# Moving the next layer's sixteen first modulation columns from the second-table stage to between the output projection panels

## The reference, cut to what matters

```python
c_act = jax.nn.silu(c)
for l in range(DEPTH):                       # DEPTH = 2
    mod = c_act @ w_mod[l] + b_mod[l]        # w_mod[l]: 1024 x 6144
    sh1, sc1, g1, sh2, sc2, g2 = jnp.split(mod, 6, axis=-1)
    h = _modulate(_rmsnorm(x), sh1, sc1)
    z = h @ w_in[l]
    ...                                      # gating, latent attention, pooling: ya, yb, yc
    merged = (gates[:, :, 0] * (ya @ w_a[l]) + gates[:, :, 1] * (yb @ w_b[l])
              + gates[:, :, 2] * (yc @ w_c[l]))
    x = x + g1[:, None, :] * (merged @ w_o[l])
    h2 = _modulate(_rmsnorm(x), sh2, sc2)
    x = x + g2[:, None, :] * _peer(h2, w_pq[l], sub_keys[l], u_tab[l], v_tab[l])
return _rmsnorm(x, final_norm)
```

## Time and profile before

| | |
|---|---|
| time, median of 3 runs | 3391.51 us (3388.35 to 3396.68) |
| the profiled execution | 3398.23 us, of which span 3396.4 us |
| PE busy | 3335.4 us, 98% of the span |
| DVE busy | 2685.5 us, 79% |
| ACT busy | 1400.9 us, 41% |
| POOL busy | 1451.2 us, 43% |
| granted clock of PE, mean | 0.987 of 2.4 GHz |
| HBM, mean over the span | 267 GB/s |

### The profile page before, as it was taken

How to read it: one execution, slowest core, us unless ns; L and a number is a source line. 1 busy time by engine, 2 the same in 40 slices (tenths; PEclk the granted TensorE clock), 3 DMA queues, 4 the chain that set the end, 5 groups by cost and what they waited for, 6 DMA issues and landing times.

```text
span 3396.4 us, 51667 instructions
## 1 busy us (share of the span) xinstructions
PE 3335.4 (98%) x16944; PEld 2905.3 (86%) x16944; DVE 2685.5 (79%) x4905; ACT 1400.9 (41%) x2298; POOL 1451.2 (43%) x1291
## 2 busy tenths in 40 slices
PE   7999999999999999999999999999999999999999
PEld 5777789999999988888877767999999998888887
DVE  6455668999888689999854556799998877899996
ACT  3334343434477433333343342443435773333333
POOL 1011106766662345566301101086767524456661
PEclk9999999999999999999999999999999999999999
DMA  6475437767799999999734744477768999999994
GB/s 228 134 253 187 150 121 221 213 206 230 228 309 327 349 393 378 399 404 402 304 129 148 241 158 154 144 221 215 214 205 260 337 320 379 361 405 399 405 400 184
DMA packets 306395, 909.86 MB, mean 268 GB/s; under 512 B 69076, under 2 KB 101892, under 8 KB 305316
## 3 DMA queue, kind: packets, MB, share of 16 engines
q0 software_dynamic: 163792, 473.58, 40.6%
q1 hardware_dynamic: 105552, 383.83, 31.8%
q10 hardware_dynamic: 36868, 50.35, 4.1%
HBM read 792.14 MB, written 115.47 MB: 267 GB/s over the span
## 4 chain that ended last, share of the span: by engine, by line
PE 91%; DVE 4%; DMA 2%; issue 1%; POOL 1%; ACT 1%; ACTq 0%; SPq 0%; DVEq 0%; POOLq 0%
PE ps L462 15%; PE ps L464 15%; PE ps L463 15%; PE ps L1076 11%; PE ps L1074 10%; PE ps L1075 10%; PE ps L1054 3%; PE ps L877 2%; PE ps L974 1%; PE ps L975 1%; PE ps L976 1%; PE ps L933 1%; PE ps L506 1%; PE ps L1014 1%; DVE urow L1693 1%
## 5 line engine op out<-in xcount | busy, mean ns | idle before, releaser
L462 PE MATMUL ps<-mov,whl 128*128 128x384 f32 (+1 forms) x2816 | 1007.7, 358 | 1.2 <-DVE whl L449 1.2
L464 PE MATMUL ps<-mov,whl 128*128 128x384 f32 (+1 forms) x2816 | 987.6, 351 | 0.0
L463 PE MATMUL ps<-mov,whl 128*128 128x384 f32 (+1 forms) x2816 | 987.0, 350 | 0.0
L449 DVE TENSOR_TENSOR whl<-raw,whl 128x1024 fp32r<-128x1024 f32 x648 | 792.0, 1223 | 183.3 <-ACT whl L439 178.7
L439 ACT CAST whl<-raw 128x1024 fp32r<-128x1024 f32 x648 | 680.1, 1050 | 100.5 <-ACT hst L1241 96.4
L1074 PE MATMUL ps<-whl,wgthl 128*128 128x512 f32 x1536 | 607.9, 396 | 2.2 <-DVE wgthl L1792 2.2
L1076 PE MATMUL ps<-whl,wgthl 128*128 128x512 f32 x1536 | 609.0, 397 | 0.0
L1075 PE MATMUL ps<-whl,wgthl 128*128 128x512 f32 x1536 | 603.7, 393 | 0.0
L462 PEld LDWEIGHTS ps<-mov,whl 128*128 128x128 f32 x2816 | 530.4, 188 | 39.4 <-issue 8.7
L464 PEld LDWEIGHTS ps<-mov,whl 128*128 128x128 f32 x2816 | 529.5, 188 | 31.6
L463 PEld LDWEIGHTS ps<-mov,whl 128*128 128x128 f32 x2816 | 530.2, 188 | 30.4 <-issue 2.2
(11 more groups left out here) (263 smaller groups left out, 3628.4 us busy)
## 6 DMA issues: line engine op xcount, KB each, us to landing
raw<-in_uT_tab SPq DMA_DIRECT2D x256, 512.0 KB, 4.1
raw<-in_v_tab SPq DMA_DIRECT2D x256, 512.0 KB, 6.8
expert_spill<-hst ACTq DMA_DIRECT2D x256, 192.0 KB
hin<-expert_spill POOLq DMA_DIRECT2D x256, 192.0 KB, 7.8
gt<-weight_spill POOLq DMA_DIRECT2D x64, 768.0 KB, 9.1
raw<-in_w_in SPq DMA_DIRECT2D x72, 512.0 KB, 11.4
raw<-in_w_mod SPq DMA_DIRECT2D x64, 512.0 KB, 3.7
weight_spill<-stage POOLq DMA_DIRECT2D x14, 2048.0 KB, 14.8
```

Of the source, the lines that this page charges most:

```text
L449: nc.vector.tensor_tensor(whl[:, m % RING, 1], raw[:, raw_n(m) % RAW], whl[:, m % RING, 0].bitcast(F32), ALU.subtract).then_inc(lo_done, 1)
L462: nc.tensor.matmul(o, w[:, 0, k], src[:, 0, k, :cols], start=(k == 0), stop=False)
L463: nc.tensor.matmul(o, w[:, 0, k], src[:, 1, k, :cols], start=False, stop=False)
L464: mm = nc.tensor.matmul(o, w[:, 1, k], src[:, 0, k, :cols], start=False, stop=(k == KC - 1))
```

## The change

The sixteen columns of the next layer are no longer loaded by POOL into `modv` and made in the V stage. They become entries `("next", i)` of `ORDER`, one behind each branch and W_o panel, so SP loads them into the slots of `raw`. DVE makes column i in the step of panel 35 + i, ahead of that step's `split_lo`: column 0 in the last input panel's step, 1 to 8 in the branch steps, 9 to 15 in the first seven W_o steps. SP's first two query heads are written out ahead of the loop, as the slots that they wait for have another order now. The sum with the bias stays where it was, at the end of the V stage.

```diff
@@ order_of_panels
-    order += [("m", m) for m in range(M_ABC, M_T)]
+    for m in range(M_ABC, M_T):
+        order += [("m", m), ("next", m - M_ABC)]
@@ module
-MOD_AT = {30 + 6 * i: i for i in range(MOD_FIRST)}
@@ SP: load, and the loop over ORDER
+                    elif kind == "next":
+                        sp.wait_ge(next_done, l * MOD_FIRST + i + 1)
...
+                elif kind == "next":
+                    src = w_mod[ds(l * N_MOD + (N_MOD + i), 1)].rearrange("o p (k c) -> p (o k) c", k=KC)
@@ SP: the query heads
-            settle(sp)
-            with sp.Fori(0, PH // 2) as two:
+            def two_heads(two, first=False):
+
                 for n in range(2 * (2 + T_U)):
...
+                    if first and n < RAW:
+                        load(l, N_HEAD + n, src)
+                        continue
...
+            two_heads(0, first=True)
+            settle(sp)
+            with sp.Fori(1, PH // 2) as two:
+                two_heads(two)
@@ POOL
-            def load_mod(i):
-                settle(pool)
-                pool.dma_start(modv[:], w_mod[ds((l + 1) * N_MOD + i, 1)].rearrange("o p k -> p (o k)")
-                               ).then_inc(modv_in, 16)
...
-                if j == DOTS_V:
-                    pool.wait_ge(dot_done, UR + l * SLOTS + SLOTS)
-                    load_mod(0)
...
-                if j - 1 in MOD_AT and MOD_AT[j - 1] + 1 < MOD_FIRST:
-                    i = MOD_AT[j - 1]
-                    pool.wait_ge(modv_done, l * MOD_FIRST + i + 1)
-                    load_mod(i + 1)
@@ DVE: new
+        def next_column(l, m):
+
+            i = m + 1 - M_ABC
+            if 0 <= i < MOD_FIRST:
+                n = RAW_OF[("next", i)]
+                dve.wait_ge(raw_in[n % RAW], l * (16 * RAW_USES) + 16 * (n // RAW + 1))
+                mod_column(mod[:, i:i + 1], raw[:, n % RAW].rearrange("p k c -> p (k c)"), next_done)
@@ DVE: steps of the input, branch and W_o panels, the same line in each
+                    next_column(l, i)
                     split_lo(dve, l, i + LEAD)
...
+                next_column(l, m)
                 split_lo(dve, l, m + LEAD)
@@ DVE: V stage
-                if j in MOD_AT:
-                    i = MOD_AT[j]
-                    dve.wait_ge(modv_in, l * (16 * MOD_FIRST) + 16 * (i + 1))
-                    settle(dve)
-                    mod_column(mod[:, i:i + 1], modv[:], modv_done)
                 if j == P - 2 and l + 1 < DEPTH:
                     dve.wait_ge(bias_in, (l + 2) * 16)
-                    dve.wait_ge(modv_done, (l + 1) * MOD_FIRST)
+                    dve.wait_ge(next_done, (l + 1) * MOD_FIRST)
```

More of the change, by code:

```diff
@@ L100 @@
 RAW_ALL = N_HEAD + M_ALL - M_T
-assert N_IN - MOD_LAG == N_MODX
+assert N_IN - MOD_LAG == N_MODX and M_T - M_ABC == MOD_FIRST
 assert RAW_ALL % RAW == 0 and N_HEAD % RAW == 0 and M_T % RING == 0 and M_ALL % RING == 0
@@ L324, in build_trunk @@
     idu = sb("idu", [P, SLOTS], U32)
-    htok_at = top_of[0]
     htok = sb("htok", [P, D])
@@ L368, in build_trunk @@
     assert free + 4 * D + 2048 + 4 * MOD0 * D <= y_at
-    modv = sb("modv", [P, D], at=htok_at)
     ps = nc.alloc_psum_tensor("ps", [P, 8, S], F32)
@@ L376, in build_trunk @@
     hi_done, lo_done, gemm_done = sem("hi_done"), sem("lo_done"), sem("gemm_done")
-    mod_done, mod0_done, modv_done, modv_in = sem("mod_done"), sem("mod0_done"), sem("modv_done"), sem("modv_in")
+    mod_done, mod0_done, next_done = sem("mod_done"), sem("mod0_done"), sem("next_done")
     mod0_in = [sem(f"mod0_in{i}") for i in range(MOD0)]
```

## The result

The change makes the kernel slower: 3409.0 us median of 7 runs (3400.25 to 3413.18) beside 3392.44 us of the kernel before (7 runs, 3388.35 to 3398.5). The ratio is 1.0043, 95% interval 1.0028 to 1.0058, or +14.6 us (9.5 to 19.7). The forecast was 3405 us, range 3396 to 3415, +13.6 us. The title names only the output projection panels, but columns 0 to 8 are made ahead of them, column 0 in the last input panel's step and 1 to 8 in the branch steps. The cost comes from these.

What follows compares the result with a forecast made beforehand. The prediction took PE's stream of matmuls to bound the kernel (91% of the chain). Per layer 4.2 + 0.4 + 2.2 = 6.8 us, 13.6 us for two layers on the 3391.5 us median, gave 3405 us, range 3396 to 3415.

Steps and rivals of the forecast that it cites:

- step 1: V stage: taking the columns and loads out gains between 0 and 2.2 us for both layers, taken as 0.
- The stretch of the matmuls by the work beside them: V stage: columns might slow their own panel's matmuls, giving back about 5 us a layer; the prediction rejected it.
- Rival (d): V stage: DVE sets the pace, so 32 columns give back 36 us, less the 13.6, making 3369 us; chance 0.07.
- step 2: Branch stage: columns 1 to 8 make DVE late, delaying PE at W_o panel 0 by 4.2 us a layer.
- Rival (b): Branch stage: DVE's lag hides, costing 0 to 2 us, 3392 us; chance 0.08.
- step 3: Last input panel's step and W_o: column 0 costs 0.4 us a layer, columns 9 to 15 cost 0.
- step 4: SP's and GpSimd's load queues: the moved loads cost 0, upper bound 8 us a layer.
- Rival (c): Branch stage: loads come late, 13.6 us plus up to 16, about 3413 to 3421 us; chance 0.10.
- step 5: W_o panel 0: PE's wait lowers its clock, costing 2.2 us a layer, bounds 0 and 2.9.
- Rival (a): W_o panel 0: the lag is there but the clock holds, +9.2 us, 3401 us; chance 0.15.

Runs made afterwards that it cites:

- run 1: Changed kernel with columns 0 and 1 in the first branch step, 2 to 15 by twos in the first seven W_o steps: 3392.23 us, 0.9996 of the kernel before.
- run 8: Kernel before, with the sixteen columns and their loads left out of the V stage and made nowhere: 3391.18 us, ratio 0.9998.
- run 5: Changed kernel with each of columns 2 to 8 computed twice in its branch step, loads unchanged: 3419.87 us, 1.0086 of the kernel before.
- run 3: Changed kernel loading only a quarter of each of columns 0 to 8, with all of DVE's work kept: 3406.24 us, 1.0050 of the kernel before.
- run 2: Changed kernel with columns 0 to 8 summing only 16 of 1024 products on DVE, loads kept: 3406.83 us, 1.0045 of the kernel before.
- run 7: Changed kernel with nine and seven purposeless matmuls ahead of PE's waits for chunks 6 and 7 of W_o panel 0: 3401.64 us, 1.0023 of the kernel before.
- run 4: Changed kernel with columns 0 to 8 loading a quarter and DVE using 16 elements of each: 3397.48 us, 1.0022 of the kernel before.
- run 6: The changed kernel measured once more, unaltered: 3409.41 us, 1.0051 of the kernel before.
- run 10: Changed kernel, columns 0 and 1 in first branch step, 2 to 15 by twos in W_o, plus purposeless matmuls in attention's tail: 3387.26 us, 0.9989 of kernel before.

## Why the prediction was right, and where not

**The V stage gives nothing (step 1): shown.** Its length is the same within 0.8 us in the kernels before and after and in runs 1 and 8, and the columns' 18 us reappear as idle time of DVE in run 8. The stretch of the matmuls by the work beside them, which would have made 5 us a layer, is refuted by run 8. Rival (d) is refuted by runs 1 and 8: without the branch stage's cost there is no gain.

**The lag in the branch stage (step 2): shown, to the tenth.** 4.2 us a layer were predicted, +4.2 measured in S, the step at 6.12 beside 6.13 us. DVE's idle time is gone from the second step's products on ("from the third step on" had been written, against its own 0.09 us of lag for column 2). Runs 5 and 3 confirm that a column is 1.14 us of DVE as soon as the 0.37 us of idle time are gone. Rival (b), that the lag hides, is refuted.

**Column 0 and columns 9 to 15 (step 3).** From the column ahead to the row maximum it is 337.60 - 327.27 = 10.33 us in the earlier trace rows; in the kernel after it is 10.63, in layer 1 10.62 beside 10.34. So 0.3 us, predicted 0.4. The W_o columns are free (run 1).

**The loads cost nothing (step 4): right in the sum, wrong as a reason, and in part luck.** I divided bytes by time and compared rates, 293 GB/s (the stage then carried 258) against 385. That isn't what decides. What decides is how long a gate takes to land beside the other loads, and the gates had 0.4 to 1.2 us to spare. With DVE's time taken away, the loads cost 3.4 and 4.9 us a layer, in the order of issues of run 2. In the kernel after the gates land later too, and it costs nothing since DVE's lag lets them be wanted 1.4 us later. Rival (c) exists as a mechanism, through `gst` and not through `raw_in`, and it is masked; its size in the kernel after is not shown. ACT's splits waited 8.3 us for panels in layer 0's branch stage of the kernel after, where they had waited for none; DVE never waited for a split there.

**The clock (step 5): right in mechanism, near in size.** PE idled 4.06 us, as "over 4" said (step 5 had some 4.5), and the clock fell. What left the clock full before was an idle time of half a microsecond, not the "half second" of step 5. The price was 1.5, 1.5, 1.9 and 2.7 us in the four passages of the kernel after, and 1.8 as a mean with runs 2 and 3 (eight passages, 1.3 to 2.7); 2.2 had been taken. Rival (a) is refuted, and run 7 shows the cause and, with T back at 40.26, the price.

**The sum.** The traces show 2 x (4.2 + 0.3 + 1.8) = 12.6 us, predicted were 13.6, timed 14.6 and 17.3. The same sum from stretches is 9.0 for run 7, timed 7.8, and 30.4 for run 5, timed 29.2. Runs 2, 3 and 4 have 12.1, 12.0 and 3.1 us from S, T and column 0, and were timed 15.3, 17.0 and 7.5. By their own traces the kernel after and run 6 have 12.1 and 13.7 us. So the traces hold 2.5 to 5 us less than the timings in the kernel after and runs 2, 3, 4 and 6, and 1 us more in runs 5 and 7. Each sum but that of run 4 lies within the interval of its timing (4.4 to 10.9 us there). That five of seven remainders point the same way may be a small further cost; if it is one, its cause is open, and that the forecast came within 1 us of the first timing is in part luck. The traces show no further stage that grew: from the last W_o residual to the first V matmul it is on average 711.5 us in the seven kernels with columns in the branch stage, and 712.3 in the three with none of the new columns. That stretch, with the same code everywhere, varies from 709.0 us (run 1, mean granted clock 1.00) to 714.3 (run 6, 0.99), and executions of one kernel vary by some 10 to 15 us.

## What to carry to other kernels

Work added to an engine off the path is free only up to the idle time that it has in each step (0.37 us here, for a column of 1.14), and that number differs by stage more than any share of busy time says: the V stage with DVE at 91% took a column in every sixth panel for nothing, and the branch stage at 82% had room for a third of one a step. Ask of a transfer how late it may land, not whether the rate suffices, and cut both bounds before calling either one the cause, since each alone can hide the other. Look whether a cut also moves the order in which loads are issued, as the one in run 2 did. Where the path gets a new wait of a few microseconds, look at the clock behind it; filling the wait with idle matmuls gave back that part, and placing the columns in W_o gave back all.

## What the runs showed of the hardware that was not expected

- A load of 256 KB issued by POOL landed in 4.5 us beside 195 GB/s of traffic in the branch stage, and in 5.9 us (at most 7.1 in layer 0, 7.6 in layer 1) beside 257 GB/s in run 2, far below the 385 GB/s carried elsewhere. Yet beside 258 GB/s in the kernel after it landed in 4.6 us (at most 5.8 in layer 0, 6.4 in layer 1): mean traffic alone doesn't set it. The order of the issues differs: the 512 KB column load went out 0.27 us ahead of the first gate in run 2, and between the second and the third gate in the kernel after. It was not tested by itself.
- Two idle times of PE of 2.32 and 1.74 us, with three matmuls between them, brought the clock from 1.00 to 0.51 (mean over 407.40 to 410.80 us). Neither of the two is long, and with matmuls put into them it stayed at 1.00 (run 7). In the kernel before, one idle time of 0.51 us left it at 1.00.
- The same fall cost 1.3 to 2.7 us in different executions. In four of the eight passages the clock was at 0.50 for a short time (407.4 to 410.6 us in the kernel after), and T grew by 1.3 to 1.5 us. In the other four it was low for longer (408.2 to 414.8 us in run 6), and T grew by 1.7 to 2.7 us.
- The attention's tail, from the last row maximum to the first gate products, lasted 13.8 to 16.0 us in the 22 passages without added matmuls, though its code is the same in all, and 12.3 in both passages of run 10 at full clock.
